# Group norm of the RWKV branch: the prompt's mean taken off by a product with the unit matrix less 1/64 per head, in place of the output's transposition; the samples' rows centred at their copy out of PSUM

## What is computed

```python
S, o = _wkv_scan(S0, r, decay, k, v, kk, a)
mean = jnp.mean(o, -1, keepdims=True)               # over the 64 channels of a head
var = jnp.mean(jnp.square(o - mean), -1, keepdims=True)
o = ((o - mean) * lax.rsqrt(var + GN_EPS)).astype(p.dtype)
o = o * gn_g.reshape(RW_HEADS, RW_HEAD) + gn_b.reshape(RW_HEADS, RW_HEAD)
o = o + jnp.sum(r * k * r_k, -1, keepdims=True) * v
o = o.reshape(B, T, RW_WIDTH) * jax.nn.silu(z)
```

## Time and profile before

| | us |
|---|---|
| median of 3 runs | 1521.59 |
| lowest and highest | 1520.94, 1523.57 |
| the profiled execution: its time | 1522.04 |
| its span, first to last instruction | 1520.4 |

### The profile page before, as it was taken

The page is one execution under the profiler, slowest core; times in us unless marked ns, Lnnn a source line. Parts: engine busy times, 40 slices in busy tenths (PEclk is TensorE's granted clock), DMA queues, the critical chain, the costliest instruction groups (busy, mean ns, idle before and its releaser), DMA issues.

```text
span 1520.4 us, 36335 instructions
## 1 busy us (share of the span) xinstructions
PE 1476.5 (97%) x14554; PEld 1075.9 (71%) x14554; DVE 849.1 (56%) x1695; ACT 552.0 (36%) x1349; POOL 332.7 (22%) x435
## 2 busy tenths in 40 slices
PE   6999999999999999999999999999999999999998
PEld 3455577767888888776777767676767777777753
DVE  3153556656777777556667676767676522023421
ACT  3056444541222222245363635454545232210000
POOL 0000140220111111124131322212131046354200
PEclk9999999999999999999999999999999999999999
DMA  9813688823465566411121212111112125352302
GB/s 326 306 45 105 165 251 274 255 80 108 126 151 153 151 155 159 116 44 32 38 57 39 53 32 52 36 48 40 44 39 57 56 84 161 83 166 73 101 14 77
DMA packets 190965, 165.42 MB, mean 109 GB/s; under 512 B 38490, under 2 KB 169562, under 8 KB 189772
## 3 DMA queue, kind: packets, MB, share of 16 engines
q1 hardware_dynamic: 181516, 127.52, 30.1%
q0 software_dynamic: 8352, 32.52, 6.9%
q10 hardware_dynamic: 928, 3.05, 0.6%
HBM read 136.97 MB, written 26.08 MB: 107 GB/s over the span
## 4 chain that ended last, share of the span: by engine, by line
PE 89%; DVE 5%; ACT 2%; DVEq 2%; issue 1%; DMA 1%; SPq 0%; POOL 0%; ACTq 0%
PE me_bank L3150 13%; PE rw_bank L1863 12%; PE sa_psOs L1218 8%; PE sa_psS L1173 7%; PE me_bank L3170 4%; PE pr_psZ L741 4%; PE fr_bankL L307 3%; PE rw_bank L1899 2%; PE pr_psS L729 2%; PE fr_bankL L247 2%; PE sa_psT L1183 2%; PE rw_bank L1875 2%; PE rw_bank L1960 2%; PE pr_psO L762 1%; PE pr_psT L752 1%; PE sa_psS L1168 1%
## 5 line engine op out<-in xcount | busy, mean ns | idle before, releaser
L1863 PE MATMUL rw_bank<-hT,big 128*128 128x288 f32 x336 | 95.2, 423 | 0.0
L1279 ACT COPY kpe<-sa_psS 128x512 f32<-128x512 f32 x64 | 34.4, 589 | 135.8 <-PE sa_psS L1173 135.8
L741 PE MATMUL pr_psZ<-hT,qlT 128*128 128x288 f32 x256 | 73.6, 407 | 0.6 <-DVE pr_zraw L845 0.6
L1017 POOL DMA_DIRECT2D big<-in_cache_kv x68 | 37.6, 553 | 154.5 <-issue 154.5
L1863 PEld LDWEIGHTS rw_bank<-hT,big 128*128 128x128 f32 x336 | 60.2, 191 | 15.7 <-issue 1.2
L3209 ACT COPY big<-me_bank 128x288 f32<-128x288 f32 x42 | 16.8, 399 | 144.8 <-PE me_bank L3150 144.8
L1017 POOL DMA_DIRECT2D pages<-in_cache_kv x68 | 37.5, 552 | 118.7 <-issue 118.7
L741 PEld LDWEIGHTS pr_psZ<-hT,qlT 128*128 128x128 f32 x256 | 46.8, 189 | 21.3 <-issue 9.5
L1218 PE MATMUL sa_psOs<-big,sa_ST 128*128 128x257 f32 x256 | 60.3, 386 | 0.0
L1218 PE MATMUL sa_psOs<-pages,sa_ST 128*128 128x257 f32 x256 | 60.3, 385 | 0.0
L1369 DVE TENSOR_TENSOR sa_ST<-sa_psT,kinvp 128x512 f32<-128x512 f32 x64 | 42.9, 679 | 30.6 <-PE sa_psT L1183 30.5
(11 more groups left out here) (629 smaller groups left out, 3671.7 us busy)
## 6 DMA issues: line engine op xcount, KB each, us to landing
big<-in_w_in SPq DMA_DIRECT2D x44, 512.0 KB, 4.0
big<-in_cache_kv POOLq DMA_DIRECT2D x68, 128.0 KB, 3.8
pages<-in_cache_kv POOLq DMA_DIRECT2D x68, 128.0 KB, 3.1
fr_wada<-in_w_ada SPq DMA_DIRECT2D x8, 1024.0 KB, 11.8
big<-in_cache_kv SPq DMA_DIRECT2D x60, 128.0 KB, 3.0
pages<-in_cache_kv SPq DMA_DIRECT2D x60, 128.0 KB, 3.0
qk_scratch<-oaT SPq DMA_DIRECT2D x32, 192.0 KB, 2.6
fr_wada<-in_w_ada SPq DMA_DIRECT2D x2, 2048.0 KB, 11.0
```

The source lines that it names most:

```text
L741: last = nc.tensor.matmul(psZ[h][:, 0:HT], M.wz[hp % 2][:, k, :], M.hT[:, k, h * HT:(h + 1) * HT], start=(k == 0), stop=(k == KT - 1))
L1017: e.dma_start(M.pages[s % 2][q * QP:(q + 1) * QP, g, :, 0:KL], src).then_inc(landed, 16)
L1279: nc.scalar.copy(S.rearrange("q (c p j) -> q p c j", c=2 * GP, p=GP)[:, :, cs, :], got[:, :, cs, :]).then_inc(copied, 1)
L1863: last = mm(into, held, moving, start=(k == 0 and n in (1, 2, 7)), stop=(k == K4 - 1), skip_group_check=True)
```

## The change

It does four things. `out_to_tokens` issues a matmul with `M.less_mean` as the moving operand in place of each transposition: the output comes out turned, and less its mean over the 64 channels of its head. `M.less_mean`, the unit matrix less 1/64 where `head_mask` is 1, is made once by VectorE ahead of the first pair's grams. `sample_out` sums the samples' rows in PSUM, multiplies by 1/64 and writes the difference, where it copied. `centre` goes, and `squares` waits for `o_sb` and `pick_sb` in place of `centred`.

```diff
             def out_to_tokens(i):
                 pe.wait_ge(oc_sb, i + 1)
+                pe.wait_ge(less_mean_sb, 1)
                 for c in range(PB):
-                    last = tr(bank[6][:, c * P:(c + 1) * P], oc_of(i)[:, c * P:(c + 1) * P], M.ident[:, :])
+                    last = mm(bank[6][:, c * P:(c + 1) * P], oc_of(i)[:, c * P:(c + 1) * P], M.less_mean[:, :], start=True, stop=True)
                 last.then_inc(oc_tr, 1)
...
             def squares(i):
-                act.wait_ge(centred, i + 1)
+                act.wait_ge(o_sb, i + 1)
+                act.wait_ge(pick_sb, i + 1)
                 a.activation(osq[:, :, :], o[:, :, :], ACT.Square).then_inc(squared, 1)
...
                 tt(uv[halves[0], :].rearrange("p (h i) -> p h i", h=2), Y[halves[0], 8:NU, RH:P], bank[5][halves[0], 0:P].rearrange("p (h i) -> p h i", h=2), ALU.add)
-                v.tensor_copy(o[halves[1], 8:NU, :], bank[5][halves[1], 0:P].rearrange("p (h i) -> p h i", h=2)).then_inc(pick_sb, 1)
+                got, mean = bank[5][halves[1], 0:P].rearrange("p (h i) -> p h i", h=2), om[halves[1], 0, 8:NU]
+                v.tensor_reduce(mean, got, AX.X, ALU.add)
                 dr()
+                ts(mean, mean, 1.0 / RH, None, ALU.mult)
+                dr()
+                tt(o[halves[1], 8:NU, :], got, bc(mean, RH, 2), ALU.subtract).then_inc(pick_sb, 1)
                 tt(uvm[:, :, :], bc(uv[:, :], BD, 1), bc(pick[:, 0:BD], P, 2), ALU.mult).then_inc(uvm_sb, 1)
 
-            def centre(i):
-                dve.wait_ge(o_sb, i + 1)
-                v.tensor_reduce(om[:, 0, :], o[:, :, :], AX.X, ALU.add)
-                dr()
-                ts(om[:, 0, :], om[:, 0, :], 1.0 / RH, None, ALU.mult)
-                dr()
-                tt(o[:, :, :], o[:, :, :], bc(om[:, 0, :], RH, 2), ALU.subtract).then_inc(centred, 1)
+            def less_mean():
+                stt(M.less_mean[:, :], head_mask[:, :], -1.0 / RH, M.ident[:, :], ALU.mult, ALU.add).then_inc(less_mean_sb, 1)
...
                 if i == 0:
                     dve.wait_ge(late_masks_in, 48)
+                    less_mean()
...
                 state(i, 3)
-                centre(i)
...
+            M.less_mean = view(slots + 2 * USED, P)
```

More of the change, by code:

```diff
@@ L1522, in rwkv @@
             sem(n) for n in ("zkv_mm", "zkv_sb", "y_mm", "y_sb", "ys_mm", "ys_sb", "zr_mm", "zr_sb", "pick_mm", "pick_sb"))
-        rt_mm, rt_sb, psi_mm, s_next, phi_mm, o_mm, o_sb, centred, squared, var, rstd, normed = (
-            sem(n) for n in ("rt_mm", "rt_sb", "psi_mm", "s_next", "phi_mm", "o_mm", "o_sb", "centred", "squared", "var", "rstd", "normed"))
+        rt_mm, rt_sb, psi_mm, s_next, phi_mm, o_mm, o_sb, less_mean_sb, squared, var, rstd, normed = (
+            sem(n) for n in ("rt_mm", "rt_sb", "psi_mm", "s_next", "phi_mm", "o_mm", "o_sb", "less_mean_sb", "squared", "var", "rstd", "normed"))
         s_tr, s0p_sb, sp_tr, sp_sb, z_mm, z_sig, z_sb, o_tr, o_read, ob_sb, uvm_sb, sn_mm, sn_sb, sn_tr, sn_out = (
```

## The result

The kernel after takes 1525.22 us in the median of 22 runs (1521.89 to 1527.84), the kernel before, measured beside it, 1523.78 us (22 runs, 1520.28 to 1526.29). The medians are 1.44 us apart (0.09%); the comparison of the two sets of runs gives a ratio of 1.0014 [1.0008, 1.0020], some 2.1 us. That is less than the 0.2% that counts as a change, but its interval excludes 1. A second comparison, in another session, gave 1.0004 [0.9994, 1.0014], which doesn't exclude it. The intervals overlap between 1.0008 and 1.0014. The forecast was +0.12%, or 1523.5 us; the 1.7 us between this and 1525.22 come from the base, since before itself was taken at 1521.59 and measured here at 1523.78. The forecast of the change is right. Its parts are right only in part, as the traces show.

A forecast was written before the change was run, and what follows sets the result against it. TensorE, 97% busy, was taken as the bound, waiting on VectorE's chain at seven boundaries. 7 x 0.17 + 0.58 + 0.1 = +1.9 us on 1521.6 gave 1523.5 us, +0.12%; range 1520.8 to 1526.0.

The forecast's parts named there:

- The record price: Products in out_to_tokens: two records each, 0.126 us a record as in line 2111; four take 1.01 us, 0.58 more than transpositions.
- the other end: Products in out_to_tokens at line 2043's 0.16 us a record: 0.85 us more; as dear-products rival +4.4 us, 1526.0, chance 0.15.
- Not fourfold: Rival for out_to_tokens: a product costs four transpositions, the four take 1.74 us; +7.7 us, 1529.3 us; chance 0.03.
- What centring holds up: Between head pairs, VectorE's centring delays masking the next pair's first grams by 0.51 us, less the hand-over, not 1.89.
- hand-over: From TensorE finishing the first grams to VectorE starting on them: 0.10 us taken, between 0.04 and 0.15.
- The boundary: At each of seven boundaries between head pairs, line 1863 starts 0.17 us later; together +1.2 us.
- The wait: TensorE's wait for VectorE before line 1863, multiply(i, VZ, 4): 0.2 to 0.3 us in place of 0.68.
- The last stretch: Last pair, after line 2105: nothing follows that centring holds up, so the products' 0.58 us go straight onto the end.
- `sample_out`: Ahead of state(i, 1): +0.6 us under 1.38 us of cover; rival that it holds up carry(i, 2): 1524.3 us, chance 0.03.
- The extra wait: Second wait in out_to_tokens, one more TensorE instruction: 0 to 0.14 us in eight pairs, 0.1 taken.

The follow-up runs named there:

- ident_product: Kernel before with four products by the unit matrix in place of the transpositions, centring kept on VectorE; ratio 1.0025, 1526.61 us beside 1523.04.
- no_centre_tr: Kernel after with the transpositions put back, so the mean of the prompt's output is not taken off; ratio 0.9981 to before, 1520.45 us.
- nine_waits: Kernel before with nine already fulfilled TensorE waits at the head of out_to_tokens; timed once, 1524.2 us beside 1523.57.

## Why the prediction was right, and where only its sum was

- *The record price.* This is the term that was mis-sized. Forecast 0.126 us from seven products in a row, measured 0.111. The four products cost 0.46 us more and not 0.58; the other end, 0.16 from line 2043, was wrong for this place. The step that two records stand for a product was right, 8 for 4 transpositions.
- *Not fourfold.* Four products take 0.89 us and four transpositions 0.43, a ratio of 2.07. The Trainium skill, "TensorE: Matmul & The Clock Gate", section "Terms", gives the transpose mode as four times faster for float32; the runs here don't agree, and ident_product would have come out at some +10 us by it, not at +3.7. (The 1.74 us that the prediction gives for the four at this price is 4 x 0.43 = 1.72; nothing rests on the difference.)
- *What centring holds up.* Forecast 0.51 us a boundary less the hand-over; no_centre_tr shows it to 0.02 us. The hand-over is 0.05 us at each boundary looked at, near the lower of the two ends (0.04 and 0.15) and not between them.
- *The boundary.* Forecast +0.17, measured 0.00. Both of its mis-sized terms, 0.12 of products and 0.05 of hand-over, erred the same way, and seven of them make the 1.2 us that the forecast has and the kernel hasn't. The wait is 0.23 us, within the 0.2 to 0.3 that was forecast.
- *The last stretch.* Forecast +0.58, measured +0.46: the mechanism was right, the size off by the record price again.
- *`sample_out`.* Forecast +0.6 us under 1.38 us of cover. In the middle pairs it is +0.56, and 0.82 is left. In the last pair, which I didn't look at, there is next to nothing left, since VectorE's instructions are longer beside GpSimd's work; it costs 0.09 us. This rival got 0.03 and is, by a tenth of a microsecond, true.
- *The extra wait.* Forecast 0.1 us; the kernels with nine and eighteen more waits show 0.00 on the shortest distance. As work, a fulfilled wait cost nothing here that could be measured.
- *What was not foreseen*: +1.05 us of standstills within the rows of 32x32 products. The view of waits had them in before, beneath the only row that I took from it, and I treated what is put down to "issue" as if it were fixed. The edits tried here shifted it by -1.4 us (nine_waits) to +1.05 (after).

So the sum of 1.9 us was made of 1.2 + 0.58 + 0.1, and the measured 1.6 is 0.00 + 0.46 + 0.09 + 1.05. That the two are near each other is luck; had the standstills come out as in nine_waits, the stage would have been 0.8 us shorter than before's, with the same boundary. The 8-in-10 range of 1520.8 to 1526.0 was wide enough to hold both. The measured interval, [1.0008, 1.0020], lies above 1.6 us in its middle (2.1); the second comparison, [0.9994, 1.0014], below it.

## What to carry to other kernels

The chain of waits named 1.89 us of VectorE work at each boundary, and 0.44 of it was worth having: compare when the engine behind it would have been able to start, had the step not been there. Before a step is moved to the busy engine, look whether an idle one can take it; GpSimd took the subtraction at no cost to the others, and the kernel was 0.18% faster, where the product made it no faster. On a stream of many small instructions, look at several pairs and at what is put down to "issue": a difference of 0.1% can be in it alone, and the shortest of the repeated distances is what shows the work.

## What the runs showed of the hardware that I had not expected

- TensorE stands still for 0.3 to 0.9 us within rows of 32x32 products, at places that stay the same from execution to execution of a kernel and move when mere waits are added; in sum 0.57 to 3.03 us of a stage of 580. 39 of 44 breaks end 1.25 to 1.52 us after a 16 KB transfer of queue q8, of the kind "instruction", has landed.
- A four-product row costs 0.111 us a record in this place, less than the 0.126 of a row of seven in the same kernel.
- A multiplication of 64x2 on VectorE took 1.01 us beside GpSimd's work, ended 0.02 us after GpSimd's instruction did, and took 0.17 without it, but masking 128x512 out of PSUM took 1.35 us beside GpSimd's subtraction of 128x640, and 1.34 without.
- After 2.23 us of standstill TensorE was granted 0.63 and 0.79 of its clock in the next 6.4 us, which cost some 1.6 us more. After 1.2 us of it in the first pair, one execution had 0.61 and 0.86 and another 1.00 throughout, with the same waits: 1.4 us of difference, ahead of the first edited product.
